# Mixer input projections: the high and low halves of a tile's two weight units made ahead of its convolution steps, turns two tiles behind, SiLU one behind

## The reference, cut to what matters

```python
h = rmsnorm(x, norm_mix_pre)
proj = h @ w_in
z, xbc, dt_raw, q, k, v = jnp.split(proj, IN_OFFSETS, axis=-1)
xbc = silu(depthwise_conv_centred(xbc, conv_w, conv_b))   # width 5
X, Bm, Cm = split(xbc, (1024, 1280))                      # 1024 + 256 + 256 features
dt = softplus(dt_raw + dt_bias)
y = ssd_scan(forward) + ssd_scan(backward) + X * d_skip   # state-space scan, chunks of 128
mix = concat(rmsnorm(y * silu(z)), window_attention(q, k, v)) @ w_out
x = x + rmsnorm(mix, norm_mix_post)
x = x + rmsnorm(square(relu(rmsnorm(x) @ w_up)) @ w_down)
```

## Time and profile before

| what | us |
|---|---|
| runs | 1144.91, 1147.14, 1149.0 (median 1147.14) |
| profiled execution | 1148.56 |
| its span | 1146.7 |
| PE busy | 1091.2 (95%) |
| DVE busy | 816.3 (71%) |
| ACT busy | 610.7 (53%) |
| GpSimd busy | 129.3 (11%) |

### The profile page before, as it was taken

One profiled execution on the slowest core, in us unless ns is written; L12 is line 12 of the kernel. 1 busy time (PEld: TensorE's weight loads), 2 busy tenths in 40 slices (PEclk: granted clock), 3 DMA queues, 4 the chain that ended last, 5 costly groups with the idle time before them and its releaser, 6 DMA issues.

```text
span 1146.7 us, 20585 instructions
## 1 busy us (share of the span) xinstructions
PE 1091.2 (95%) x7226; PEld 984.1 (86%) x7226; DVE 816.3 (71%) x1288; ACT 610.7 (53%) x1058; POOL 129.3 (11%) x139
## 2 busy tenths in 40 slices
PE   8989999999999999999999999897788898999997
PEld 7978999999788997779999998897666787999996
DVE  6758877776743567878777776999877557666664
ACT  6657444444756846656444446544347746444443
POOL 0230111111010012201111110101502200000000
PEclk9999999999999999999999999999899899999999
DMA  8254665655555655435655563554000273655541
GB/s 337 90 190 141 209 197 187 192 192 183 173 194 165 190 179 177 151 111 165 201 184 199 185 201 111 184 184 147 1 9 28 93 222 126 200 184 185 188 157 37
DMA packets 51382, 185.09 MB, mean 161 GB/s; under 512 B 5728, under 2 KB 6240, under 8 KB 51328
## 3 DMA queue, kind: packets, MB, share of 16 engines
q1 hardware_dynamic: 49248, 178.28, 47.2%
q0 software_dynamic: 1504, 5.44, 1.4%
q10 hardware_dynamic: 576, 0.64, 0.2%
HBM read 183.28 MB, written 1.05 MB: 161 GB/s over the span
## 4 chain that ended last, share of the span: by engine, by line
PE 85%; DVE 8%; ACT 4%; issue 2%; DMA 0%; DVEq 0%; SPq 0%; ACTq 0%
PE ps L208 26%; PE ps L166 17%; PE ps L167 17%; PE ps L168 17%; DVE w_lo L149 2%; DVE arena L1556 1%; PE ps L667 1%; PE ps L696 1%; DVE a_lo L389 1%; ACT a_hi L383 1%; ACT arena L720 1%; PE ps L680 1%; PE ps L1466 1%; PE ps L230 1%; PE ps L933 1%
## 5 line engine op out<-in xcount | busy, mean ns | idle before, releaser
L149 DVE TENSOR_TENSOR w_lo<-raw,w_hi 128x1024 fp32r<-128x1024 f32 x336 | 420.3, 1261 | 141.3 <-ACT w_hi L144 141.1
L144 ACT ACTIVATE w_hi<-raw 128x1024 fp32r<-128x1024 f32 x336 | 347.5, 1054 | 170.6 <-PE ps L168 104.0
L166 PE MATMUL ps<-a_hi,w_hi 128*128 128x256 f32 x1408 | 400.8, 285 | 4.6 <-DVE arena L354 3.0
L167 PE MATMUL ps<-a_lo,w_hi 128*128 128x256 f32 x1408 | 399.1, 283 | 0.0
L168 PE MATMUL ps<-a_hi,w_lo 128*128 128x256 f32 x1408 | 399.1, 283 | 0.0
L166 PEld LDWEIGHTS ps<-a_hi,w_hi 128*128 128x128 f32 x1408 | 270.6, 192 | 9.2 <-DVE arena L354 3.1
L167 PEld LDWEIGHTS ps<-a_lo,w_hi 128*128 128x128 f32 x1408 | 270.7, 192 | 2.5
L168 PEld LDWEIGHTS ps<-a_hi,w_lo 128*128 128x128 f32 x1408 | 270.6, 192 | 0.0
L208 PE MATMUL ps<-w_hi,a_hi 128*128 128x512 f32 x496 | 161.9, 400 | 8.2 <-DVE a_lo L1138 2.9
L208 PE MATMUL ps<-w_lo,a_hi 128*128 128x512 f32 x496 | 157.4, 390 | 0.0
L208 PE MATMUL ps<-w_hi,a_lo 128*128 128x512 f32 x496 | 157.3, 390 | 0.0
(11 more groups left out here) (184 smaller groups left out, 1071.4 us busy)
## 6 DMA issues: line engine op xcount, KB each, us to landing
raw<-in_w SPq DMA_DIRECT2D x336, 512.0 KB, 4.2
row<-in_rows POOLq DMA_DIRECT2D x7, 512.0 KB, 4.1
x<-in_x SPq DMA_DIRECT2D x2, 512.0 KB, 4.3
out<-x SPq DMA_DIRECT2D x4, 256.0 KB, 2.1
misc<-in_misc POOLq DMA_DIRECT2D x1, 512.0 KB, 6.0
arena<-in_ws POOLq DMA_DIRECT2D x1, 512.0 KB, 7.4
tab<-in_tables POOLq DMA_DIRECT2D x1, 320.0 KB, 4.8
tab<-in_tables POOLq DMA_DIRECT2D x1, 256.0 KB, 5.0
```

What stands on the lines that cost most here:

```text
L144: act.activation(w_hi[:, s, :], raw[:, s, :], ACT.Copy).then_inc(hi_done, 1)
L149: dve.tensor_tensor(w_lo[:, s, :], raw[:, s, :], w_hi[:, s, :].bitcast(F32), ALU.subtract).then_inc(lo_done, 1)
L166: pe.matmul(o, l_hi, r_hi, start=first, stop=False)
L167: pe.matmul(o, l_hi, r_lo, start=False, stop=False)
```

## The change

On ACT and DVE the halves of both units of a tile are made together. SiLU of tile j is written one turn of the loop later (the last behind the loop), the query product of tile j at the top of the next turn of the loop, and PE turns tile j - 2 instead of j - 1. The scan on PE waits for all twelve SiLUs instead of all twelve copies.

```diff
 # mixer_in_pe
-            if 1 <= j < XT - 1:
-                turn(j - 1)
+            if 2 <= j < XT:
+                turn(j - 2)
 # mixer_in_act
-        for j in range(XT):
-            if j == 0:
-                dt_move_act(act)
-            hi_to(act, x_unit(j) + 5)
-            if 2 <= j < XT:
-                move(j - 2)
-            hi_to(act, x_unit(j) + 6)
-            if j == 0:
-                dt_act(act)
-                act.preload_act_table(ACT.Silu)
+        def silu(j):
             act.wait_ge(x_sem.conv, 5 * j + 5)
             if 2 <= j < 8:
                 act.wait_ge(x_sem.turned, j - 1)
             act.activation(xbc_dst(j), S_CV[:, j % 2, :], ACT.Silu).then_inc(x_sem.silu, 1)
+
+        for j in range(XT):
+            if j == 0:
+                dt_move_act(act)
+            hi_to(act, x_unit(j) + (6 if j < QKT else 5))
+            if 2 <= j < XT:
+                move(j - 2)
+            if j >= 1:
+                silu(j - 1)
+            if j == 0:
+                dt_act(act)
+                act.preload_act_table(ACT.Silu)
+        silu(XT - 1)
         decay_act(act)
 # mixer_in_dve
+        def query(j):
+            ...  # the wait and the product that stood at the end of the loop
         for j in range(XT):
-            lo_to(dve, x_unit(j) + 5)
+            if 1 <= j <= QKT:
+                query(j - 1)
             if j == 0:
+                lo_to(dve, x_unit(0) + 5)
                 row_dve(dve, 4, 2)
                 dt_before()
             ...
             dve.tensor_tensor(pad[:, b, 2:2 + SEQ], ps[:, x_bank(j), 0:SEQ], ROW, ALU.mult).then_inc(x_sem.copied, 1)
+            lo_to(dve, x_unit(j) + (6 if j < QKT else 5))
             ...  # the five steps of the convolution
-            lo_to(dve, x_unit(j) + 6)
-            if j < QKT:
-                ...  # wait and query product
 # ssd_pe
         pe.wait_ge(x_sem.moved, XT - 2)
-        pe.wait_ge(x_sem.copied, XT)
+        pe.wait_ge(x_sem.silu, XT)
         pe.wait_ge(at2.qk, QKT)
```

More of the change, by code:

```diff
@@ L1275, in mixer_in_dve @@
                               ALU.mult).then_inc(q.v, 1)
+        def query(j):
+            dve.wait_ge(unit_used, x_unit(j) + 2)
+            dst = A_Q[:, j, :] if j < QT else A_K[:, j - QT, :]
+            dve.scalar_tensor_tensor(dst, ps[:, 2 + j % 2, 0:SEQ], DH ** -0.5 if j < QT else 1.0, ROW,
+                                     ALU.mult, ALU.mult).then_inc(q.qk, 1)
         dt_before, dt_between, dt_behind = dt_dve(dve)
         for j in range(XT):
-            lo_to(dve, x_unit(j) + 5)
+            if 1 <= j <= QKT:
+                query(j - 1)
             if j == 0:
+                lo_to(dve, x_unit(0) + 5)
                 row_dve(dve, 4, 2)
```

## The result

The changed kernel takes 1149.39 us (median of 12 runs, 1148.11 to 1151.2) against 1147.2 us for the kernel before (12 runs, 1144.91 to 1149.53). The ratio is 1.0021, 95% interval 1.0013 to 1.003: 2.2 us slower by the medians, 2.4 by the ratio, inside 0.3% but clear of the scatter. The profiled execution took 1150.48 us with a span of 1148.7; before it was 1148.56 and 1146.7.

The account below looks back on a forecast made before the run. TensorE was taken to bound the middle, by 0.45 us per pair; front and middle gave 0, the back +1.3, so profiled 1148.56 became 1149.9, less 1.42 to the run median: 1148.4 us, range 1145.6 to 1151.3.

Parts of the forecast that it names:

- Front: Start of the projections, tile 0: TensorE's 2.99 us idle before its second unit stays, so 0.
- Middle: Projections' loop: work per tile the same on each engine, TensorE stays at 5.98 us per pair, no new wait: 0.
- One turn fewer: TensorE up to the end of tile 10's conv unit: one turn fewer done, -0.22 us, copy of tile 10 at 787.98.
- (a): VectorE, tiles 10 and 11: low half of 251 moves behind copy 10 (+1.2), copy 11 at 791.98, conv steps from 794.1.
- (b): Convolution of tile 11: overlap with GpSimd's masks gone, steps take 2.05 instead of 3.55, SiLU starts at 796.15: -0.5 us.
- (c): VectorE's scan start: high half of unit 253 slips behind SiLU, table load and decay exponential, +1.65 to +2.5 us.
- (d): First quarter of the scan: VectorE's 1.16 us idle absorbs part, second half starts at 805.4: +1.3 (+0.5 to +2.2).
- (e): TensorE at the scan's start: at the full clock it stays under VectorE's 805.4; at the low clock +2.2 us.
- The rule that was weighed: GpSimd beside VectorE in the scan: full-length exclusion would give +3.3 instead of the 0.83 charged, 1150.8 us.
- Even: Rival, chance 0.21: tile 11's conv collisions are not paid again, GpSimd's masks falling beside VectorE's idle time: 1146.8 us.
- Slower by over 0.3%: Rival, chance 0.11: TensorE's clock stays low in the scan's first quarter, also third quarter's state product: +4.0, 1151.1 us.
- Faster by the front: Rival, chance 0.05: the waits at the front go, 2.99 us idle plus half-clock time, 4.2 in all: 1142.9 us.

Follow-up runs that it names:

- e3: Changed kernel, with ScalarE's high half of unit 253 made ahead of SiLU of tile 11 instead of behind the decay exponential: 1146.07 us, ratio 0.9991.
- e5: Changed kernel, with the high half of unit 253 ahead of SiLU of tile 11 and the row of scales copied first: 1142.49 us, ratio 0.9969.
- e6: Kernel before, with the row of scales copied first and TensorE's turns two tiles behind: 1146.12 us, ratio 0.9986.
- e7: Kernel before, with only TensorE's turns two tiles behind: 1147.07 us, ratio 1.0006.
- e1: Kernel before, with the halves of unit 253 made behind the projections' loop (ScalarE's behind the decay exponential): 1149.4 us, ratio 1.0021.
- e2: Kernel before, with only TensorE's wait ahead of the scan changed from copy to SiLU of tile 11: 1147.0 us, ratio 0.9998.
- e12: Changed kernel, high half of 253 before tile 11's SiLU, scales row first, 20 identity products before scan, decays at tile 9, low half of 253 later: 1143.54 us.
- e4: Kernel before, with the row of scales and first step-size instructions put ahead of VectorE's two low halves at tile 0: 1147.46 us, ratio 1.0005.
- e9: Changed kernel, with only the row of scales copied first at the front: 1145.26 us, ratio 0.9979.
- e8: Changed kernel, high half of 253 before tile 11's SiLU, low half of 251 before tile 10's copy, TensorE's scan first waiting for copy 11, SiLU 10: 1148.19 us.
- e10: Changed kernel, high half of 253 before tile 11's SiLU, scales row first, 20 unread identity products on TensorE before the scan: 1142.22 us, ratio 0.9959.

## Why the prediction was right, and where a size was off

The forecast was 1148.4, a little slower and no change to be told; it is 1149.39, 2.2 slower instead of 1.3. The timed runs can tell it, since their interval is 0.001 to each side and not the 0.3% that I allowed.

**Front, 0.** Right: 2.97 us of idle time. In the two profiles A is 0.7 longer after, with a longer stretch of low clock (below). e3 has the same front as the changed kernel and A is 72.70, so this is not the change. That the step of 0.41 us showed a low clock was misread: the clock was 1.00 until 726 and fell just behind it, and a first step behind a wait takes 0.38 at 1.00 as well (at 719.18).

**Middle, 0.** Right in effect: TensorE's pair is 5.98 us (788.42 - 782.44). One sentence in it was wrong: that the work per tile is the same for VectorE. The work is, the time is not. Its period is 5.34 us instead of 5.53. Of the 0.19, 0.12 lie behind the copy: the convolution's first step, which needs its result, began 0.45 behind it, and now a low half, which does not, begins 0.33 behind it (746.81 and 747.14). TensorE hid it here; with the front mended (e5 against e6) it is worth part of 1.4 us in A. The line of before:

```profile
752.85 0.42 DVE L1289 TENSOR_SCALAR arena<-pad,cols 128x256 f32<-128x256 f32 x1
```

**One turn fewer, -0.2.** e7's A is 0.2 shorter; below what the timed runs tell.

**(a), (b).** From the copy of tile 10 to that of tile 11 3.88 us (predicted 4.00), the convolution steps 5.79 behind copy 10 (6.1), 2.05 long (2.05). SiLU starts 7.87 behind copy 10, 8.49 before: -0.6, predicted -0.5.

**(c).** The mechanism is the one named, shown two ways: by e1 on the kernel before (+2.2), and by e3 against the changed kernel (-3.4). In the place itself VectorE waits 2.96 us and begins the scan 11.94 behind copy 10, before 10.47: +1.5, just below the +1.6 to +2.5 of my sign. The low half began at 799.22, 0.14 ahead of GpSimd's first mask, and took 1.23: the collision that I charged to it (0.83) did not fall there, since the masks waited for differences at the low clock; it fell on the next instructions instead.

**(d), (e): the mis-sized term.** I gave the back +1.3, and e1 shows 2.2 for the late high half alone. The step that was off is (d): it let the delay eat VectorE's 1.16 us of idle time ahead of the second half. In e1 that idle time is still 1.15, because the second half waits for exponentials that stand behind TensorE's first state product, and this product stands behind VectorE's own scaled inputs: a later start of VectorE moves both. (e) had that path, at the full clock below (d) and at the low one at +2.2, and I took the full clock; but the product had been at the low clock before as well (2.08). So the low clock there is no price of the change: 2.08, 2.07 in e1, 2.07 after. (Small in this: by the distance of before, 799.57 - 798.67 = 0.90, the scaled inputs would have been ready at 802.1 and not at 801.9.) In the changed kernel's profile the state product starts 14.52 behind copy 10, before 11.42: +3.1, of which 1.5 are the late start and 1.6 two collisions ahead of it (next paragraph). The second half starts 18.80 behind copy 10, before 15.87: +2.9.

That the profile shows 2.9 there and the timed runs 2.2 to 2.4 over the whole is not resolved. At the last products of the scan the changed kernel's profile is 3.5 us behind the other (847.37 against 843.89), and its span is only 2.0 longer. But the 1.5 us are an oddity of the profile before: from those products to the end of the span it took 302.8 us, and 301.1 to 301.7 in the other thirteen profiles. My rival's second price, a third quarter's state product at the low clock (2.08 at 826.82), was paid in this profile, but the second and fourth ran at the full clock instead, 1.12 each. e2, where the same wait alone made no difference in the timed runs, speaks against the clock as the change's price on average. The Trainium skill, TensorE: Matmul & The Clock Gate, Part 1, says of the slow stretch at a kernel's start that its length varies from run to run of one kernel. The traces agree for the stretch behind the front's idle time, where both kernels have the same TensorE instructions: the clock is below 1.00 in the four microseconds from 726 to 730 before (0.60, 0.50, 0.50, 0.69) and in eight from 724 to 732 after (0.66, six times 0.50, 0.93); in the five experiments with the old front it is four or five.

**The rule that was weighed.** By the rows a collision cost VectorE 0.83 us, by the rule of the Trainium skill (SBUF — State Buffer, Who interferes with whom) GpSimd's whole instruction. The first scan instruction, 0.17 us of work, took 1.00; the scaled inputs 1.49 for 0.69; the first weighted exponentials 2.45 for 2.19; together 1.9 us for three GpSimd instructions, between the 0.83 charged and the 3.3 of the rule. The first two, 1.6 us, stand ahead of TensorE's state product; the third does not. In e12 one group lost 4.04 us beside 5.5 us of GpSimd's work (795.57 to 801.12), more than any single collision and less than the whole length. I should have charged more than one collision.

**The rivals.** Even: not met, the collisions were paid again. Slower by over 0.3%: no; its sign, a state product of 2 us, was met, but it was met before the change too and so could not tell the two apart. Faster by the front: the change does not touch it, but e4, e5 and e9 show what the row was worth: 4 us of A, and nothing if it is removed alone.

Open: what the order in the loop is worth alone. e8 does not show it, since its tail is neither that of before nor that of e3; against its 1 us above before, its profile shows a start of the scan 0.7 later. Open too is how much of e5's gain over e6 is VectorE's period and how much the tail.

## What to carry to other kernels

When a loop that prepares data ahead is given another bound, list for every engine which item the last turn now leaves unmade and what the next request for it stands behind: here one conversion of 1.05 us slipped behind SiLU, a table load and the decays, and cost 2.2 us alone. When a delay meets idle time further on, ask what that idle time waits for: if it waits for something that the delay moves too, it hides nothing (1.15 us in e1, 1.16 before). A reordering that removes a wait off the critical path showed no gain by itself here; look for the stall on the critical engine, remove it, and see whether the new wait that takes its place is the one that the reordering removes. For effects of 1 to 3 us read distances between fixed events, and compare the same code in several profiles before explaining a difference.

## What the runs showed of the hardware

A collision added about the same to a short VectorE instruction as to a long one, where both it and GpSimd's read two inputs from the same memory: the one of 0.17 us took 1.00 beside a GpSimd mask (L1543 at 800.36, and again at 825.04), the scaled inputs of 0.69 took 1.49, and the low half of 1.23 took 2.06. A low half that had begun 0.14 us ahead of the mask (799.22 and 799.36) kept its 1.23, and the two masks took 2.98 instead of 2.22. And keeping TensorE busy with 20 products (4.63 us in e12) in its idle time did hold the full clock (1.00, and 1.95 us for 16 products instead of 3.62, in e10 and e12), with no difference in the time of the kernel that can be told.
